# The squares of the third convolution chunk, summed in two fp32r passes instead of one plain fp32 matmul

## The reference, cut to what matters

```python
conv = gate_b * short_conv(gate_c * conv_in, w_conv[i])

mix = jnp.concatenate([group_rms_norm(attn, g_attn_out[i], N_HEADS),
                       group_rms_norm(conv, g_conv_out[i], CONV_GROUPS)], axis=-1)
x = x + rms_norm(mix @ w_out[i], g_post_mix[i])
```

## Time and profile before

| | us |
|---|---|
| median of 3 runs | 2715.26 |
| lowest, highest | 2714.13, 2715.74 |
| the profiled execution | 2714.51 |
| its span, first to last instruction | 2712.7 |
| PE busy | 2693.9 (99%) |
| DVE busy | 2035.9 (75%) |
| ACT busy | 1398.7 (52%) |
| POOL busy | 302.9 (11%) |

### The profile page before, as it was taken

The page is one execution under the profiler, slowest core; times in us unless marked ns, Lnnn a source line. Parts: engine busy times, 40 slices in busy tenths (PEclk is TensorE's granted clock), DMA queues, the critical chain, the costliest instruction groups (busy, mean ns, idle before and its releaser), DMA issues.

```text
span 2712.7 us, 34642 instructions
## 1 busy us (share of the span) xinstructions
PE 2693.9 (99%) x12840; PEld 2239.6 (83%) x12840; DVE 2035.9 (75%) x2757; ACT 1398.7 (52%) x2401; POOL 302.9 (11%) x329
## 2 busy tenths in 40 slices
PE   8999999999999999999999999999999999999999
PEld 7888888888888888888888888888888888888886
DVE  5468888476787777798865788893867787777986
ACT  5337888564333333346644478884633333333464
POOL 0230000001111111110003200000011111111000
PEclk9999999999999999999999999999999999999999
DMA  4211112532111111133232111133311111111422
GB/s 166 78 67 42 34 34 73 184 109 71 62 47 55 39 58 52 63 117 117 86 116 76 60 41 34 29 134 129 140 45 49 63 47 55 39 56 54 148 94 78
DMA packets 85943, 206.19 MB, mean 76 GB/s; under 512 B 8976, under 2 KB 37776, under 8 KB 84752
## 3 DMA queue, kind: packets, MB, share of 16 engines
q1 hardware_dynamic: 85776, 203.97, 22.3%
HBM read 172.42 MB, written 31.52 MB: 75 GB/s over the span
## 4 chain that ended last, share of the span: by engine, by line
PE 96%; DVE 3%; ACT 1%; issue 0%; DMA 0%; SPq 0%; ACTq 0%
PE ps L1133 28%; PE ps L1135 28%; PE ps L1134 28%; PE ps L1339 4%; PE ps L1364 2%; PE ps L1363 2%; DVE nm L2380 1%; PE ps L1172 0%; PE ps L1173 0%; DVE ptl L2387 0%; DVE wl L2142 0%; PE ps L1304 0%; PE ps L1200 0%; ACT hh L1648 0%; PE ps L1159 0%; PE ps L1158 0%
## 5 line engine op out<-in xcount | busy, mean ns | idle before, releaser
L1133 PE MATMUL ps<-hh,wh 128*128 128x512 f32 x2160 | 848.5, 393 | 8.1 <-DVE hl L2178 8.1
L1135 PE MATMUL ps<-hh,wl 128*128 128x512 f32 x2160 | 841.2, 389 | 0.0
L1134 PE MATMUL ps<-hl,wh 128*128 128x512 f32 x2160 | 841.2, 389 | 0.0
L1648 ACT ACTIVATE wh<-raw 128x256 fp32r<-128x256 f32 (+2 forms) x510 | 319.2, 631 | 440.9 <-PE ps L1135 315.4
L2142 DVE TENSOR_TENSOR wl<-raw,wh 128x256 fp32r<-128x256 f32 (+2 forms) x510 | 380.2, 758 | 159.6 <-ACT wh L1648 159.3
L1133 PEld LDWEIGHTS ps<-hh,wh 128*128 128x128 f32 x2160 | 405.8, 188 | 95.2 <-DVE wl L2142 8.3
L1134 PEld LDWEIGHTS ps<-hl,wh 128*128 128x128 f32 x2160 | 405.9, 188 | 87.0 <-issue 3.6
L1135 PEld LDWEIGHTS ps<-hh,wl 128*128 128x128 f32 x2160 | 405.7, 188 | 84.8
L2568 DVE TENSOR_TENSOR xf<-xf,ps 128x1024 f32<-128x1024 f32 x280 | 337.3, 1214 | 35.8 <-PE ps L1135 34.4
L1133 PE MATMUL ps<-hx,wh 128*128 128x512 f32 x448 | 174.6, 390 | 0.6 <-DVE xf L2568 0.5
L1135 PE MATMUL ps<-hx,wl 128*128 128x512 f32 x448 | 174.3, 389 | 0.0
(11 more groups left out here) (238 smaller groups left out, 4294.2 us busy)
## 6 DMA issues: line engine op xcount, KB each, us to landing
raw<-w_units SPq DMA_DIRECT2D x170, 512.0 KB, 3.4
raw<-w_units SPq DMA_DIRECT2D x112, 256.0 KB, 2.9
x_mid<-xf SPq DMA_DIRECT2D x4, 2048.0 KB, 7.9
xf<-x_mid SPq DMA_DIRECT2D x4, 2048.0 KB, 7.7
hh<-mix_hi SPq DMA_DIRECT2D x14, 512.0 KB, 6.2
hl<-mix_lo SPq DMA_DIRECT2D x14, 512.0 KB, 7.4
stage<-w_head SPq DMA_DIRECT2D x16, 320.0 KB, 3.4
mix_hi<-cyh SPq DMA_DIRECT2D x8, 512.0 KB, 2.6
```

The lines of the kernel that those rows point to most:

```text
L1133: nc.tensor.matmul(dst, ah, bh, start=start, stop=False)
L1134: nc.tensor.matmul(dst, ah, bl, start=False, stop=False)
L1135: return nc.tensor.matmul(dst, al, bh, start=False, stop=stop)
L1648: return nc.scalar.activation(dst, src, ACT.Copy, **more)
```

## The change

One number: the third chunk (j = 2) is now also below `TWO_PASS`. The waits on `cv_sq_lo` and `cv_sq_hi` count by it and follow.

```diff
 CHUNKS = CONV // P
 FIRST_AT = [0, 2, 4, 6]
-TWO_PASS = 2
+TWO_PASS = 3
 TAIL_BANKS = (4, 5, 7, 0, 1, 2)
```

## The result

The changed kernel is slower: 2725.95 us in the median (2725.87 to 2726.69, 5 runs) against 2715.15 (2714.13 to 2715.74, 5 runs). The ratio is 1.0040, with a 95% interval of 1.0029 to 1.0051. That is 10.8 us. The sign and the place were forecast, the size wasn't: 7.0 us were, and the time lies 0.15 us above the upper end of the range. The profiled execution took 2726.28, its span is 2724.5 against 2712.7.

What follows compares the result with a forecast made beforehand. PE was taken as the bound with next to no slack; 4.3 us of waiting less 0.79 saved, about 3.5 a layer, made 7.0, so 2715.26 + 7.0 = 2722.3 us, range 2720.4 to 2725.8.

Steps and rivals of the forecast that it cites:

- The bound: Whole run: PE busy 2693.9 of 2712.7 us, next to no slack, so waiting put into its list is lost.
- What PE saves: Chunk 2 sums on PE: 1.16 us in place of 1.95, saving 0.79 a layer, 1.6 for both.
- When the operands are ready: Copies wait behind `kh`, subtractions behind `kl`; `cvs_r` starts about 189.05, PE's first pair 189.79, idle 3.95 us.
- The sum: Sums of chunk 2: 4.3 us waiting less 0.79 saved, about 3.5 lost a layer, 7.0 for both.
- rival 1: PE's matmuls behind the wait also run at half clock: 2725.4 if both waits do it, 2723.8 with one; chance 0.2.
- its longer form: Half-clock matmuls behind PE's wait, with the slow stretch lasting twice as long as at the start: 2728 us.
- Rival 2: Later PE waits shrink and give back 1 to 3.9 us: 2718.4 to 2721.3; chance 0.12.
- Rival 3: At the sums no wait arises and the edit gains its 1.6 us: 2713.7; chance 0.03.
- The sign of PE's busy time: Whole run: PE's busy time falls, if anything, while its idle time grows by about 8 us.

Runs made afterwards that it cites:

- the two kernels with late sums: Chunk 2 sums one output later (CSTAT_AT[2] = 32): on the changed kernel 2713.20 us, on the kernel before with plain sums 2714.78 us.
- the filled wait: Changed kernel plus 17 matmuls of no use on PE ahead of the sums' wait: 2722.13 us, ratio 1.0025 to the kernel before.
- one of 3.29 with nothing else changed: Kernel before, plain sums of chunk 2 made to wait for DVE's second rotary-key subtraction (kr_lo): 2725.82 us, ratio 1.0039.
- The stops of 1.30 us: Kernel before, plain sums of chunk 2 made to wait for DVE's finished rotary key (kr_f): 2718.46 us, ratio 1.0012.
- the first experiment: Changed kernel with the sums of chunk 2 one output later on PE (CSTAT_AT[2] = 32): 2713.20 us, ratio 0.9993 to the kernel before.
- the stop of 2.48 us: Kernel before, plain sums of chunk 2 made to wait for ACT's second copy kh (kr_hi): 2722.00 us, ratio 1.0025.
- the kernels with 2.0 to 2.5 us of idle time: Changed kernel with parts made earlier, 2718.82 us; with 8 matmuls ahead of the wait, 2724.24; kernel before waiting for kr_hi, 2722.00.

## Why the prediction was right in its place and wrong in its size

- **The bound** (PE, no slack). Right: PE has a new wait of 7.9 us, and no other of its larger waits changed by more than 0.1.
- **What PE saves**, 0.79 us a layer. Right: 1.6 us between the two kernels with late sums, which differ in nothing but the form. It is the whole worth of the edit.
- **When the operands are ready.** Right: `cvs_r` was put at 189.05 and is at 189.11, PE's restart at 189.79 and is at 189.86, the idle time of 3.95 is 3.96. The lists of ACT and DVE and the durations of the old trace were enough for that.
- **The sum**, 3.5 us a layer. It is the right price of the delay, as the filled wait shows (7.1 measured), but not of the change: PE's pace behind the wait stands in it at its usual 0.23 us a matmul, a term of nothing, and the medians put 3.8 us there.
- **The step that failed** is the choice between the forecast and rival 1. I gave the clock's fall 0.2, on the ground that the wait is half as long as the one at the start and comes behind 180 us of dense work. Neither helped. A stop of 3.96 us made the clock fall in both layers, and so did one of 3.29 with nothing else changed. The rule of the Trainium skill ("TensorE: Matmul & The Clock Gate", section "HAM oscillation — how this bites in real kernels"), that waits between groups of matmuls throw the array back to half its clock, holds for the two waits of the changed kernel, with 0.50 granted behind both. The stops of 1.30 us had no such effect (1.00).
- **The price of rival 1** was close but small. It took one fall at the 1.54 us of the start, 3.1 for both; the medians show 3.8, and the slow stretch of the profiled execution lasts 6.1 and 5.2 us against the 3.1 that the prediction counted at the start. So rival 1's 2725.4 became 2725.95. With this rival rated as the likeliest, its 2725.4 would have been the forecast; the range of the prediction, cut at 2725.8 to leave out its longer form, missed by 0.15.
- **Rival 2** (given back). Wrong: the small waits of PE are the same rows with the same sizes.
- **Rival 3** (no wait). Its condition was right, and the first experiment meets it in another way: moving the sums one output on puts the kernel 1.9 us ahead in the medians, of which 1.6 are this rival's and 0.3 can't be told from nothing.
- **The sign of PE's busy time.** Wrong in a small thing: it was to fall, and rose from 2693.9 to 2697.8, since the records are longer at half the clock (0.63 against 0.39).

## What to carry to other kernels

Where PE is the bound, an edit that makes its operand cheaper but adds a step to another engine is to be priced by when that step's turn comes in the other engine's list; here the 1.6 us of cheaper matmuls came with 8.6 us of waiting, 7.0 net, because the copies and the subtractions stood behind an unrelated wait. A stop of PE has a second price beside its length: three to four us of standing still cost some two more at half the clock, in each layer. Either put the dependent matmuls behind the next independent unit, which takes both away, or, if the delay can't be avoided, break it with matmuls of no use, which takes away the second. Where they stand counts: 17 that fill the wait and 6 in its middle kept the clock at 1.00, and 8 at its start left one stop of 2.16 us, behind which the clock fell in both layers of the profiled execution.

## What the runs showed of the hardware that I had not expected

- A stop of 3.3 us behind 180 us (first layer) or some 1340 us (second, counted from the first stop) of dense matmuls is enough for the clock to be granted at 0.50 in both layers. The load before it did not protect.
- The fall can come during the stop (0.77 in the stretch 188 to 190 of the changed kernel) or after PE is back: in the kernel with 8 matmuls in the wait, the granted clock in steps of 0.2 us drops about 0.4 us behind PE's restart in the first layer (190.61) and 1.5 us behind it in the second (1537.77).
- Behind the stop of 2.48 us the clock fell in one layer and not in the other, in one execution, and the times of the kernels with 2.0 to 2.5 us of idle time spread by 2.5 to 3.8 us, against 1.6 for the kernel with 1.3 us of it. The kernel before spreads by 2.4 over its first 25 runs, so the spread alone proves little; the two outcomes in one execution do.
- At the very start of a run the matmuls are 0.43 us apart while the column of the granted clock shows 1.00; behind the stops of the changed kernel the same spacing goes with 0.50. The spacing of the starts is the safer sign of the two.
